# First slab of each normed stage in plain float32 from the residual, and a rebuilt gated recurrence, in a 22-stage network on one core

## The chip, the cores and the metric

The kernel runs on one core of a Trainium2 chip. The metric is the device time of one execution in microseconds. Times are of the whole program, and every time below is from runs of the kernel before the change or from the trace of its profiled execution.

## The reference, cut to what matters

The input is one sequence of 256 tokens of width 1024. It goes through residual blocks: y = x + gate * f(norm(x)). A stage that begins with a norm is called a normed stage here; there are ten. Everything is float32, and the kernel keeps near-float32 accuracy.

```python
def rms_norm(x, g):
    y = x32 * lax.rsqrt(jnp.mean(x32 * x32, axis=-1, keepdims=True) + EPS)
    return y * g
def modulate(x, g, shift, scale):
    return rms_norm_2(x, g) * (1.0 + scale[:, None, :]) + shift[:, None, :]
def rglru_mixer(h, ...):                      # the gated recurrence
    gate, xr = jnp.split(h @ w_in, 2, axis=-1)
    xr = causal_dwconv(xr, conv_w, conv_b)    # 4 taps
    r = sigmoid(xb @ w_a + b_a); i = sigmoid(xb @ w_x + b_x)   # per block of 128
    a = exp(-8 * r * softplus(-lam)); b = sqrt(-expm1(2 log a)) * (i * xr)
    h_t = a_t h_{t-1} + b_t                   # scan over the 256 tokens
    return (gelu(gate) * hs) @ w_out
```

The norm's factor 1/sqrt(mean + eps) is one number for each token, so it may be applied to the matmul's result as well as to its input: (x * g * r) @ W = ((x * g) @ W) * r. With a modulation, shift @ W has to be added after that.

## The kernel before, in words

**Layout.** Activations lie transposed: channels on the 128 partitions, the 256 tokens (T) along the free axis. The residual X is 8 tiles of 128x256 (KD = 8). All weights come from memory as 272 slabs of 128x2048 floats (1 MB), in the order in which the stages use them; slab n goes to raw[n % 4], loaded by SyncE four ahead. N0[stage] is the number of a stage's first slab.

**Three matmuls for one.** TensorE (PE) takes fp32r operands, which hold fewer bits than float32. So every slab is split on chip: ScalarE (ACT) copies it to hi in fp32r (split_hi, L1018, two halves of 128x1024), VectorE (DVE) makes lo = raw - hi (split_lo, L1485, two halves). Activations are split in the same way to XH and XL (after a norm), or HH and HL (hidden values). A product is hi*XH + hi*XL + lo*XH (three, L341 to L343), so a slab of 16 blocks of 128x128 is 48 matmuls of 256 columns. In the stages with a modulation (gated_slab) hi takes XH and XL in one matmul of 512 columns (L410) and lo one of 256 (L412). hi and lo have two buffers (n % 2): slab n+2 can be split once slab n is used.

**A stage boundary.** At the end of a down-projection DVE adds the results to X pair by pair (residual). ACT squares the tiles of X (L1046) into S; DVE folds the first four squares (L1504). norm() on PE then sums squares over channels (12 float32 matmuls of 64 columns, L535, 24 records in the trace, since a float32 matmul is recorded as two), issues 8 matmuls whose result nobody reads (busy, L522), ACT takes the square root (L1051), DVE the reciprocal, and a float32 matmul of 256 columns spreads the factor to all partitions (L543, into bank 4). DVE then makes S = X * gain * factor (L1569), ACT XH (L1057, or L1059 with the shift), DVE XL (L1560, L1562), tile by tile. The stage's first slab (first_up_slab L394 and L402, or gated_stage L439 and L446) follows these tiles as they come. Its hi and lo were made during the residual.

**The recurrence.** Stage rg_in has 10 slabs. Each holds 128 columns of gate and the same 128 of xr side by side. For each slab ACT takes gelu of the gate half (L1240) and starts the convolution of the other (L1244), DVE adds three taps (L1830), PE multiplies by the two block matrices (gates, L685 and L687, float32), ACT takes two tanh (L1230, L1232). After the last slab ACT runs tanh and exp for all ten tiles (L1253, L1256), then all square roots (L1261); DVE then runs product, scan, product, cast and subtraction (L1847 to L1851) tile by tile, and only after the tenth splits the slabs of rg_out. rg_out waits for the values so made (h_ready).

The engines run their own instructions in program order and wait on semaphores. What an engine waits for holds back all that stands behind it.

## Time and profile before

| what | value |
|---|---|
| runs | 1857.72, 1857.73, 1859.61 us, median 1857.73 |
| profiled execution | 1854.29 us, of which the span is 1852.5 us |
| mean granted TensorE clock | 0.982 |
| PE / weight loads / DVE / ACT busy | 96% / 89% / 75% / 53% |
| largest single wait of PE | 20.2 us, before rg_out |

The span is cut in the profile into matmuls (PE), weight loads (PEld) and the other engines. Matmuls overlap their successors in the trace, so a distance from start to start is the cost of one, not its own duration. The granted clock is 1.0 at 2.4 GHz and 0.5 at 1.2 GHz.

### The profile page before, as it was taken

The numbers are of one execution on the slowest core, as the hardware profiler recorded it, in microseconds if no ns is written. First come the engines' busy times: TensorE is split into PE (matmuls) and PEld (weight loads), VectorE is DVE, ScalarE is ACT, GpSimd is POOL, SyncE is SP. The second block draws the span as 40 slices with busy tenths as digits, with TensorE's granted clock in tenths as the row PEclk, the third lists the DMA queues.
The fourth block names the chain that finished last, engine by engine and source line by source line (L and its number), as shares of the span: only waits on it lengthen the run. The fifth ranks groups of instructions, "written<-read, shape, count | busy, mean of one in ns | idle before, by whom it ended". The sixth has DMA issues, their size and how long they took to land.

```text
span 1852.5 us, 31866 instructions
## 1 busy us (share of the span) xinstructions
PE 1770.9 (96%) x12854; PEld 1646.0 (89%) x12854; DVE 1384.8 (75%) x2169; ACT 974.4 (53%) x1495; POOL 16.5 (1%) x22
## 2 busy tenths in 40 slices
PE   7899999948999999999998999999999999899999
PEld 7699999948999988899997698889988999588899
DVE  4668887767888788888975867888788865856663
ACT  5455544562555365536565835553555445655542
POOL 0200000000000000000000000000000000000000
PEclk9999999978999999999999999999999999999999
DMA  8235468422445957795553035779577834035552
GB/s 346 92 109 188 181 228 307 162 99 91 162 181 185 367 201 290 272 350 196 183 182 124 14 128 195 281 282 344 215 282 281 320 141 179 2 113 187 199 182 91
DMA packets 62154, 367.16 MB, mean 198 GB/s; under 512 B 6912, under 2 KB 7040, under 8 KB 27360
## 3 DMA queue, kind: packets, MB, share of 16 engines
q1 hardware_dynamic: 61488, 362.69, 53.0%
q0 software_dynamic: 560, 3.01, 0.4%
q8 instruction: 72, 1.18, 0.3%
q14 instruction: 34, 0.28, 0.0%
HBM read 364.63 MB, written 1.05 MB: 197 GB/s over the span
## 4 chain that ended last, share of the span: by engine, by line
PE 85%; DVE 9%; ACT 4%; issue 1%; DMA 1%; SPq 0%; DVEq 0%; ACTq 0%
PE psum L410 17%; PE psum L341 17%; PE psum L343 16%; PE psum L342 16%; PE psum L412 8%; DVE lo L1485 2%; DVE S L1569 1%; PE psum L394 1%; ACT hi L1018 1%; PE psum L535 1%; DVE XHL L1562 1%; PE psum L733 1%; PE psum L805 1%; DVE tiny L1701 1%; PE psum L402 1%
## 5 line engine op out<-in xcount | busy, mean ns | idle before, releaser
L1485 DVE TENSOR_TENSOR lo<-raw,hi 128x1024 fp32r<-128x1024 f32 x542 | 641.3, 1224 | 247.0 <-ACT hi L1018 246.4
L1018 ACT ACTIVATE hi<-raw 128x1024 fp32r<-128x1024 f32 x542 | 543.3, 1051 | 456.4 <-PE psum L343 431.3
L410 PE MATMUL psum<-XHL,hi 128*128 128x512 f32 x1344 | 471.0, 397 | 1.7 <-DVE lo L1485 1.7
L341 PE MATMUL psum<-XHL,hi 128*128 128x256 f32 x1400 | 399.5, 285 | 2.2 <-DVE lo L1485 2.0
L342 PE MATMUL psum<-XHL,hi 128*128 128x256 f32 x1400 | 396.6, 283 | 0.0
L343 PE MATMUL psum<-XHL,lo 128*128 128x256 f32 x1400 | 396.6, 283 | 0.0
L341 PE MATMUL psum<-HH,hi 128*128 (+1 forms) x1328 | 382.4, 288 | 6.5 <-DVE lo L1485 6.5
L342 PE MATMUL psum<-HL,hi 128*128 (+1 forms) x1328 | 380.2, 286 | 0.0
L343 PE MATMUL psum<-HH,lo 128*128 (+1 forms) x1328 | 380.0, 286 | 0.0
L412 PE MATMUL psum<-XHL,lo 128*128 128x256 f32 x1344 | 375.2, 279 | 0.0
L410 PEld LDWEIGHTS psum<-XHL,hi 128*128 128x128 f32 x1344 | 252.4, 188 | 63.3 <-DVE lo L1485 2.5
L341 PEld LDWEIGHTS psum<-XHL,hi 128*128 128x128 f32 x1400 | 268.9, 192 | 5.4 <-issue 3.0
L342 PEld LDWEIGHTS psum<-XHL,hi 128*128 128x128 f32 x1400 | 268.9, 192 | 0.2
L343 PEld LDWEIGHTS psum<-XHL,lo 128*128 128x128 f32 x1400 | 268.9, 192 | 0.0
L341 PEld LDWEIGHTS psum<-HH,hi 128*128 128x128 f32 x1328 | 259.3, 195 | 7.4 <-issue 6.8
L342 PEld LDWEIGHTS psum<-HL,hi 128*128 128x128 f32 x1328 | 259.3, 195 | 0.1
L343 PEld LDWEIGHTS psum<-HH,lo 128*128 128x128 f32 x1328 | 259.2, 195 | 0.0
L412 PEld LDWEIGHTS psum<-XHL,lo 128*128 128x128 f32 x1344 | 253.5, 189 | 0.0
L1586 DVE CUSTOM_DVE_ANT_0 modw<-modw,cond 128x1024 f32<-128x1024 f32 x144 | 173.9, 1220 | 11.6 <-DMA modw<-wmod_dram 11.6
L1113 ACT ACTIVATE S<-psum 128x512 f32<-128x512 f32 x88 | 52.6, 598 | 220.2 <-PE psum L412 220.2
L1657 DVE TENSOR_TENSOR S<-psum,S 128x512 f32<-128x512 f32 x88 | 60.9, 692 | 72.5 <-ACT S L1113 72.4
L1626 DVE SCALAR_TENSOR_TENSOR S<-psum,PAR,S 128x254 f32<-128x254 f32 (+1 forms) x176 | 72.5, 475 | 0.0
(294 smaller groups left out, 1661.1 us busy)
## 6 DMA issues: line engine op xcount, KB each, us to landing
raw<-slabs_dram SPq DMA_DIRECT2D x270, 1024.0 KB, 4.8
modw<-wmod_dram SPq DMA_DIRECT2D x144, 512.0 KB, 5.7
A<-small_dram POOLq DMA_DIRECT2D x1, 1536.0 KB, 13.2
X<-x_dram SPq DMA_DIRECT2D x4, 256.0 KB, 3.8
raw<-slabs_dram SPq DMA_DIRECT2D x2, 512.0 KB, 6.3
out_dram<-X SPq DMA_DIRECT2D x4, 256.0 KB, 2.4
cond<-cvec_dram POOLq DMA_DIRECT2D x1, 512.0 KB, 7.2
A<-tab_dram POOLq DMA_DIRECT2D x1, 512.0 KB, 15.3
```

The source lines that it names most:

```text
L341: mm(dst, wh, xh, start=start, stop=False, skip_group_check=True)
L342: mm(dst, wh, xl, start=False, stop=False, skip_group_check=True)
L343: return mm(dst, wl, xh, start=False, stop=False, skip_group_check=True)
L394: mm(b[:, m * T:(m + 1) * T], w[:, k, at], XH[:, kt, :], start=(m == 0 and i == 0 and w is hi), stop=False, skip_group_check=True)
L410: mm(dst, hi[:, k, j * P:(j + 1) * P], XHL[:, kt, :, :].rearrange("p a t -> p (a t)"), start=start, stop=False, skip_group_check=True)
L412: return mm(dst[:, T:2 * T], lo[:, k, j * P:(j + 1) * P], XHL[:, kt, 0, :], start=False, stop=False, skip_group_check=True)
L1018: f(hi[:, n % SPLIT, at], raw[:, n % RAW, at], ACT.Copy).then_inc(q["hi_ready"], 1)
L1113: f(S[:, 1024 + s % 2 * 512:1536 + s % 2 * 512].rearrange("p (a t) -> p a t", a=2), psum[:, b:b + 2, T:2 * T], ACT.Copy).then_inc(q["half_ ...
L1485: v.tensor_tensor(lo[:, n % SPLIT, at], raw[:, n % RAW, at], hi[:, n % SPLIT, at].bitcast(F32), ALU.subtract).then_inc(q["lo_ready"], 1)
L1586: v.tensor_tensor_reduce(out=w, in0=w, in1=cond[:, :], scale=1.0, scalar=0.0, op0=ALU.mult, op1=ALU.add, accum_out=MOD[:, n:n + 1]).then_i ...
L1626: last = stt(out=z, in0=bank[n % 4][:, m * T:(m + 1) * T - tap], scalar=col(f"fconv{layer}", (2 - tap) * 44 + k, i, 4), in1=z, op0=ALU.mul ...
L1657: v.tensor_tensor(two(dst), psum[:, b:b + 2, 0:T], two(S[:, 1024 + s % 2 * 512:1536 + s % 2 * 512]), ALU.add).then_inc(evacuated[s % 2], 1)
```

## The change

Slabs in FIRST, the first of each of the ten normed stages, are no longer split. PE multiplies the raw slab, as float32, by XG = X * gain (or by XGS, which also has two columns with the shift, 258 columns in all), 16 matmuls (raw_slab). The sum of squares and the spread stand between them; DVE folds all squares, so the sum takes 4 matmuls instead of 12; the busy matmuls are gone. ACT writes XG between the squares. The spread factor is kept in SBUF (row_kept), and DVE multiplies the first slab's result by it (unscaled); with a shift, ACT then adds it as a bias. The stage's second slab takes the place that the first had: it follows XH and XL tile by tile (paced_slab). hi and lo alternate over split slabs only (SPLITS). The load of slab n+4 behind a slab in FIRST waits for that slab's use instead of its split. pa_in loads 8 columns of parameters ahead of slab 0.

In the recurrence the slabs hold first xr (5 slabs of two tiles) and then the gate (5 slabs). The convolution and the gate matmuls run in the first half; tanh, exp and the arguments of the roots run beside the slabs of the second half; then come five roots, five gelus, scans, products, HH by ACT instead of DVE, and HL, in pairs of tiles, with the splits of rg_out between them.

```diff
+FIRST = [N0[_name] for _name in ("pa_in", "f0_up", "rg_in", "f1_up", "g00_up", "ssd_in", "g01_up", "g10_up",
+                                 "mla_in", "g11_up")]
+SPLITS, HALVED = [], []
+for _n in range(NSLABS):
+    SPLITS.append(len(HALVED))
+    if _n not in FIRST:
+        HALVED.append(_n)
...
+                if n - RAW in FIRST:
+                    sp.wait_ge(q["slab_used"], n - RAW + 1)
+                else:
+                    sp.wait_ge(q["lo_ready"], 2 * (SPLITS[n - RAW] + 1))
+                sp.dma_start(raw[:, k, :], slabs[n]).then_inc(raw_loaded[k], 16)
...
+            def raw_slab(stage, dst, wide=T, bank_of_sums=3):
+
+                n, k = N0[stage], norms[0]
+                norms[0] += 1
+                source = XG if wide == T else XGS
+                sums = bank[bank_of_sums]
+
+                def part(kt, ms=(0, 1)):
+                    pe.wait_ge(q["xg_ready"], KD * k + kt + 1)
+                    for m in ms:
+                        at = slice((m * KD + kt) * P, (m * KD + kt + 1) * P)
+                        last = mm(dst(m), raw[:, n % RAW, at], source[:, kt, 0:wide],
+                                  start=(kt == 0 and (m == 0 or wide > T)), stop=False, skip_group_check=True)
+                    return last
+
+                def column_sums():
+                    pe.wait_ge(q["squares_folded"], k + 1)
+                    for m in range(2):
+                        for j in range(2):
+                            last = mm(sums[:, j * WIDE:(j + 1) * WIDE], S[:, m * T + j * P:m * T + (j + 1) * P],
+                                      ones[:, 0:WIDE], start=(m == 0 and j == 0), stop=False, skip_group_check=True)
+                    last.then_inc(q["sum_ready"], 1)
+
+                def spread():
+                    pe.wait_ge(q["diag_ready"], k + 1)
+                    mm(bank[4][:, 0:T], ones, R[:, 0:T], start=True, stop=True).then_inc(q["spread_ready"], 1)
+
+                if n == 0:
+                    column_sums()
+                    pe.wait_ge(q["slab_begun"], 16)
+                    for kt in range(KD):
+                        part(kt, (0,))
+                    spread()
+                    pe.wait_ge(raw_loaded[0], 16)
+                    for kt in range(KD):
+                        last = part(kt, (1,))
                 else:
-                    pe.wait_ge(q["xh_ready"], KD * (norms[0] - 1) + kt + 1)
...
+                    pe.wait_ge(raw_loaded[n % RAW], 16 * (n // RAW + 1))
                     for kt in range(KD):
...
+                        last = part(kt)
+                        if kt == 2:
+                            column_sums()
+                        if kt == 4:
+                            spread()
...
+                raw_slab(stage, lambda m: psum[:, m, 0:T + 2], T + 2, bank_of_sums)
+                paced_slab(N0[stage] + 1, preps,
+                           lambda m, half, w, x_, first: mm(psum[:, 2 + m, half:half + T], w, x_,
+                                                            start=(first and half == 0), stop=False,
+                                                            skip_group_check=True),
+                           lambda m, w, x_: mm(psum[:, 2 + m, T:2 * T], w, x_, start=False, stop=False,
+                                               skip_group_check=True))
+                pe.wait_ge(q["row_kept"], norms[0])
...
+            def gates(u):
+
+                pe.wait_ge(*up_count("rg_in", u))
+                for t in (2 * u, 2 * u + 1):
+                    if t >= 4:
+                        pe.wait_ge(q["it_ready"], t - 3)
+                    at = t * T
+                    mm(bank[4 + t % 4][:, 0:T], SW[:, 4 + t, :], S[:, at:at + T], start=True, stop=False,
+                       skip_group_check=True)
+                    mm(bank[4 + t % 4][:, T:2 * T], SW[:, 14 + t, :], S[:, at:at + T], start=False,
+                       stop=True, skip_group_check=True).then_inc(q["ri_ready"], 1)
...
+            def split_hi(n, i=None, ahead=False):
+
+                if n in FIRST:
+                    n += 1
+                if n >= NSLABS or n - 2 in FIRST and not ahead:
...
+                if shift is not None:
+
+                    if k:
+                        act.wait_ge(q["resid_ready"], 8 * (k - 1) + 2)
+                    f(XGS[:, :, T:T + 2], MOD[:, at:at + 8].rearrange("p (a t) -> p a t", t=1).to_broadcast([P, KD, 2]),
+                      ACT.Copy)
+
+                def scaled(kt):
+                    if shift is None:
+                        f(XG[:, kt, :], X[:, kt, :], ACT.Copy, scale=col(gain, kt)).then_inc(q["xg_ready"], 1)
+                    else:
+                        f(XGS[:, kt, 0:T], X[:, kt, :], ACT.Copy,
+                          scale=MG[:, at // 3 + kt:at // 3 + kt + 1]).then_inc(q["xg_ready"], 1)
+
                 for m, w in ((0, 2), (2, 2), (4, 2), (6, 1), (7, 1)):
...
+                    if k and m < 6:
+                        scaled(m)
+                        scaled(m + 1)
                 if k == 0:
-                    split_hi(0)
+                    act.wait_ge(q["gain_loaded"], 16)
+                for kt in range(6 if k else 0, KD):
+                    scaled(kt)
                 act.wait_ge(q["sum_ready"], k + 1)
                 f(tiny[:, 52:54], bank[bank_of_sums][:, 0:2 * WIDE:WIDE], ACT.Sqrt, scale=1.0 / D,
                   bias=tiny[:, 59:60]).then_inc(q["norm_ready"], 1)
-                split_hi(N0[stage] + 1)
+                if k == 0:
+                    split_hi(1)
+                else:
+                    split_hi(n + 2, ahead=True)
...
+            def decays(u):
+
+                for t in (2 * u, 2 * u + 1):
+                    f(TH[:, t, :], A1[:, t, :], ACT.Tanh, scale=c4[:, t:t + 1],
+                      bias=c4[:, t:t + 1]).then_inc(q["act_steps"], 1)
+                for t in (2 * u, 2 * u + 1):
+                    act.wait_ge(q["act_steps"], 1 + t + 1)
+                    f(A1[:, t, :], A1[:, t, :], ACT.Exp, scale=c4[:, RNN + t:RNN + t + 1],
+                      bias=c4[:, RNN + t:RNN + t + 1]).then_inc(q["rg_exp"], 1)
...
+                if 1 <= s <= 5:
+                    gate_tanhs(2 * s - 2)
+                    gate_tanhs(2 * s - 1)
+                if s >= 5:
+                    if s == 5:
+                        act.wait_ge(q["it_ready"], RNN)
+                    decays(s - 5)
+            act.wait_ge(q["rg_evacuated"], 5)
+            for u in range(5):
+                act.wait_ge(q["rg_arg"], u + 1)
+                f(TH[:, 2 * u:2 * u + 2, :], TH[:, 2 * u:2 * u + 2, :], ACT.Sqrt).then_inc(q["rg_root"], 1)
+            for u in range(5):
+                f(GG[:, 2 * u:2 * u + 2, :], GG[:, 2 * u:2 * u + 2, :],
+                  ACT.Gelu_apprx_tanh).then_inc(q["rg_gate"], 1)
+            for u in range(5):
+                act.wait_ge(q["rg_state"], u + 1)
+                f(HH[:, 2 * u:2 * u + 2, :], GG[:, 2 * u:2 * u + 2, :], ACT.Copy).then_inc(q["rg_high"], 1)
+                if u >= 2:
+                    split_hi(N0["rg_out"] + u)
+            split_hi(N0["rg_out"] + 5)
+
...
+            def unscaled(z, banks):
+
+                dve.wait_ge(q["row_kept"], norms[0])
+                row = R[:, T:2 * T].rearrange("p (a t) -> p a t", a=1).to_broadcast([P, 2, T])
+                return v.tensor_tensor(two(z), banks, row, ALU.mult)
...
+                for m in tiles:
+                    dve.wait_ge(q["squares_ready"], 8 * k + m + 2)
+                    last = v.tensor_tensor(S[:, 0:2 * T], S[:, 0:2 * T], S[:, m * T:(m + 2) * T], ALU.add)
+                    if m == 6:
+                        last.then_inc(q["squares_folded"], 1)
+                    else:
+                        step.link(last)
...
+                split_lo(N0[stage] + (2 if k else 1), halves=(0,), ahead=True)
...
+            def scans(u):
+                dve.wait_ge(q["rg_root"], u + 1)
+                step.link(v.tensor_tensor(tiles(TH, u), tiles(TH, u), tiles(IX, u), ALU.mult))
+                for t in (2 * u, 2 * u + 1):
+                    last = v.tensor_tensor_scan(IX[:, t, :], A1[:, t, :], TH[:, t, :], 0.0, ALU.mult, ALU.add)
+                step.put(last)
+
+            def product(u):
+                dve.wait_ge(q["rg_gate"], u + 1)
+                step.wait(step.n)
+                v.tensor_tensor(tiles(GG, u), tiles(GG, u), tiles(IX, u), ALU.mult).then_inc(q["rg_state"], 1)
+
+            def rest(u):
+                dve.wait_ge(q["rg_high"], u + 1)
+                v.tensor_tensor(tiles(HL, u), tiles(GG, u), tiles(HH, u).bitcast(F32),
+                                ALU.subtract).then_inc(q["h_ready"], 1)
+
+            scans(0)
+            scans(1)
+            product(0)
+            product(1)
+            for u in range(5):
+                rest(u)
+                if u >= 2:
+                    split_lo(N0["rg_out"] + u)
+                if u + 2 < 5:
+                    scans(u + 2)
+                    product(u + 2)
```

First place: PE at the boundary from f1_down to g00_up, the fifth norm. `CN,S` is the sum of squares, `R,CN` the spread. Before:

```order
L343 MATMUL psum<-HH,lo 128x256
L535 MATMUL psum<-CN,S 128x64 [waits squares_folded]
L535 MATMUL psum<-CN,S 128x64 x3
...
L522 MATMUL psum<-maskr,identr 128x256 x8
L543 MATMUL psum<-R,CN 128x256 [waits diag_ready]
L522 MATMUL psum<-maskr,identr 128x256 x4
L439 MATMUL psum<-XHL,hi 128x256 [waits xh_ready,lo_ready]
```

Now, at the same place:

```order
L362 MATMUL psum<-HH,lo 128x256
L411 MATMUL psum<-XGS,raw 128x258 [waits xg_ready,raw_loaded1]
...
L419 MATMUL psum<-CN,S 128x64 [waits squares_folded]
L419 MATMUL psum<-CN,S 128x64 x3
L411 MATMUL psum<-XGS,raw 128x258 [waits xg_ready]
...
L425 MATMUL psum<-R,CN 128x256 [waits diag_ready]
L411 MATMUL psum<-XGS,raw 128x258 [waits xg_ready]
...
L504 MATMUL psum<-XHL,hi 128x256 [waits xh_ready,lo_ready]
```

Six of the sixteen float32 matmuls stand ahead of the sum, four between sum and spread, six behind the spread; what waited for XH there is now the second slab.

Second place: DVE at the same boundary, from the reciprocal on. Before:

```order
L1552 TENSOR_SCALAR R<-CN,tiny 128x128
L1569 SCALAR_TENSOR_TENSOR S<-X,MG,psum 128x256 [waits spread_ready]
...
L1562 SCALAR_TENSOR_TENSOR XHL<-S,MOD,XHL 128x256 [waits xh_ready] x3
L1485 TENSOR_TENSOR lo<-raw,hi 128x1024 [waits hi_ready] x2
L1657 TENSOR_TENSOR S<-psum,S 128x512 [waits half_kept]
```

Now:

```order
L1726 TENSOR_SCALAR R<-CN,tiny 128x128
L1647 TENSOR_TENSOR lo<-raw,hi 128x1024 [waits hi_ready]
L1744 SCALAR_TENSOR_TENSOR S<-X,MG,psum 128x256 [waits spread_ready]
...
L1737 SCALAR_TENSOR_TENSOR XHL<-S,MOD,XHL 128x256 [waits xh_ready] x3
L1647 TENSOR_TENSOR lo<-raw,hi 128x1024 [waits hi_ready]
L1654 TENSOR_TENSOR S<-psum,R 128x512 [waits row_kept,half_kept]
```

One half of a slab's split went ahead of the wait for the spread, the other stayed behind the tiles, and it is now the stage's third slab that it belongs to.

Third place: ACT from the last gate slab of the recurrence to the first values for rg_out. Before, the tail of it:

```order
L1256 ACTIVATE A<-A,c 128x256 [waits act_steps]
L1261 ACT_TABLE_LOAD
L1261 ACTIVATE S<-S 128x256 [waits rg_arg] x10
L1018 ACTIVATE hi<-raw 128x1024 [waits slab_used,raw_loaded1]
```

Now:

```order
L1079 ACTIVATE hi<-raw 128x1024
L1391 ACTIVATE GG<-psum 128x512 [waits slab_used]
L1367 ACTIVATE TH<-A,c 128x256 x2
L1371 ACTIVATE A<-A,c 128x256 [waits act_steps] x2
L1403 ACT_TABLE_LOAD [waits rg_arg]
L1403 ACTIVATE TH<-TH 128x512 [waits rg_evacuated]
L1403 ACTIVATE TH<-TH 128x512 [waits rg_arg] x4
L1405 ACT_TABLE_LOAD
L1405 ACTIVATE GG<-GG 128x512 x5
L1409 ACTIVATE HH<-GG 128x512 [waits rg_state] x3
L1079 ACTIVATE hi<-raw 128x1024 [waits slab_used,raw_loaded1]
```

Eight of the ten tanh and exp pairs went ahead beside the slabs; the gelus and the copies to HH joined the tail.

## Rows read from the trace of the kernel before

**Rows 1.** Page, the chain that ended last: shares of the span by engine.
```profile
PE 85%; DVE 9%; ACT 4%; issue 1%; DMA 1%; SPq 0%; DVEq 0%; ACTq 0%
```

**Rows 2.** Windows from a stage's last matmul to its successor's third slab; after the colon: length, busy time by engine.
```profile
318.91:337.63 18.72, 17.80 (x141) 16.95 (x140) 14.86 (x30) 11.31 (x21) 0.00 (x0) 1.00 0.37 143
456.77:474.56 17.79, 17.04 (x137) 16.37 (x136) 14.90 (x31) 11.09 (x20) 0.00 (x0) 1.00 0.36 126
653.36:671.69 18.33, 16.94 (x121) 15.46 (x120) 15.64 (x30) 11.68 (x20) 0.00 (x0) 1.00 0.36 121
846.22:864.99 18.77, 17.12 (x137) 16.35 (x136) 16.75 (x35) 11.64 (x20) 0.00 (x0) 1.00 0.34 129
...
sum 165.35, PE 153.74 PEld 144.19 DVE 138.06 ACT 101.40 POOL 0.00; mean PE 17.08 PEld 16.02 DVE 15.34 ACT 11.27 POOL 0.00
```

**Rows 3.** Timeline of PE at g00_up: start us, us, what, idle before.
```profile
654.65 2.00 PE L535 MATMUL psum<-CN,S 128*128 128x64 f32 x16 [0.17 <-ACT S L1046]
...
657.72 0.70 PE L543 MATMUL psum<-R,CN 128*128 128x256 f32 x2
```

**Rows 4.** Timeline of ACT at the same boundary.
```profile
650.01 1.28 ACT L1039 ACT_TABLE_LOAD   x1
...
651.41 1.14 ACT L1046 ACTIVATE S<-X 128x512 f32<-128x512 f32 x2
...
658.98 1.31 ACT L1059 ACTIVATE XHL<-S,MOD 128x256 fp32r<-128x256 f32 x3
```

**Rows 5.** Timeline of DVE at the same boundary.
```profile
652.58 0.69 DVE L1504 TENSOR_TENSOR S<-S 128x512 f32<-128x512 f32 x1 [1.02 <-ACT S L1046]
...
658.46 1.26 DVE L1569 SCALAR_TENSOR_TENSOR S<-X,MG,psum 128x256 f32<-128x256 f32 x3 [0.79 <-PE psum L543]
...
663.58 1.27 DVE L1562 SCALAR_TENSOR_TENSOR XHL<-S,MOD,XHL 128x256 fp32r<-128x256 f32 x3
664.77 2.35 DVE L1485 TENSOR_TENSOR lo<-raw,hi 128x1024 fp32r<-128x1024 f32 x2
```

**Rows 6.** Timeline of PE: float32 matmuls of 256 columns, then fp32r ones.
```profile
389.93 0.60 PE L685 MATMUL psum<-S,A 128*128 128x256 f32 x2
390.36 0.59 PE L687 MATMUL psum<-S,A 128*128 128x256 f32 x2
...
430.99 0.28 PE L342 MATMUL psum<-HL,hi 128*128 128x256 f32 x1
431.11 0.28 PE L343 MATMUL psum<-HH,lo 128*128 128x256 f32 x1
```

**Rows 7.** Waits of PE from 390 to 440 us: us in total, times, longest.
```profile
PE psum L495 <- DVE HL L1851: 20.2, 1, 20.2
PE psum L341 <- DVE lo L1485: 5.6, 1, 5.6
PE psum L685 <- DVE S L1830: 4.2, 1, 4.2
```

**Rows 8.** Timeline of ACT in the recurrence's tail.
```profile
410.15 0.60 ACT L1256 ACTIVATE A<-A,c 128x256 f32<-128x256 f32 x1
410.76 1.28 ACT L1261 ACT_TABLE_LOAD   x1
412.06 3.17 ACT L1261 ACTIVATE S<-S 128x256 f32<-128x256 f32 x10
```

**Rows 9.** Timeline of DVE in the recurrence: three taps.
```profile
393.55 1.51 DVE L1830 SCALAR_TENSOR_TENSOR S<-psum,PAR,S 128x255 f32<-128x255 f32 x3
```

**Rows 10.** Windows in rg_out; the number behind the five engines is the granted clock.
```profile
418.00:422.00 4.00, 4.00 (x21) 4.00 (x21) 3.76 (x10) 0.00 (x0) 0.00 (x0) 0.50 0.00 0
436.00:444.00 8.00, 6.97 (x37) 7.00 (x38) 4.29 (x4) 0.00 (x0) 0.00 (x0) 0.58 0.58 230
```

**Rows 11.** Timeline of ACT and PE at the program's start: split of slab 1, use of slab 1.
```profile
13.96 2.00 ACT L1018 ACTIVATE hi<-raw 128x1024 fp32r<-128x1024 f32 x2 [0.81 <-DMA raw<-slabs_dram]
...
23.61 0.28 PE L341 MATMUL psum<-XHL,hi 128*128 128x256 f32 x1
```

More of the change, by code:

```diff
@@ L991, in _ @@
                       next_spread, key_ready)
-            up_stage("mla_out", 12)
-            norm(6)
-            gated_stage("g11_up", 13)
+            paced_up(N0["mla_out"], 12, shift=MLA_SHIFT)
+            for s in range(1, 4):
+                up_slab("mla_out", s)
+            pe.wait_ge(q["resid_ready"], RESID["mla_out"] + 4)
+            gated_stage("g11_up", 13, 6)
             down_stage("g11_down")
@@ L1279, in _ @@
             act.wait_ge(q["mod_ready"], 2)
-            norm("ssd_in", 0, 24, then=ACT.Silu)
+            norm("ssd_in", None, 0, 24, then=ACT.Silu)
             def ssd_silu(c):
@@ L1462, in _ @@
             act.wait_ge(q["mod_ready"], 6)
-            norm("g11_up", 1, 48, 6, ACT.Silu)
+            norm("g11_up", None, 1, 48, 6, ACT.Silu)
             gated_ffn("g11_up")
```

494 lines of the change are left out of this document (270 added, 224 removed).

## The prediction

> **What bounds the kernel now.** I read the chain that ended last first. It is PE for 85% of the span, DVE for 9% and ACT for 4% [rows 1], so time is won where PE waits or works for nobody. The windows show where, at the stage boundaries. From the last matmul of a stage to the first of the next stage's third slab pass 18.33 us at g00_up and 18.77 us at ssd_in, and 165.35 us in all nine boundaries after the first norm [rows 2]. Two slabs take 48 matmuls each, and fp32r matmuls of 256 columns start 0.12 us apart [rows 6]: 11.5 us. The other 6 to 7 us are norm sums, filler matmuls and waits.
>
> The timeline of PE at g00_up shows one such wait: the sums end at 656.65, and the spread starts only at 657.72 [rows 3]. The list of waits adds the recurrence: 20.2 us ahead of rg_out, 5.6 us inside it for a split that DVE has behind its scans, 4.2 us for the last taps [rows 7].
>
> **A boundary with the change.** I set zero at the start of the last matmul, 653.36 for g00_up [rows 2].
>
> The price of the float32 slab comes first. Two float32 matmuls of 256 columns start at 389.93 and 390.36, 0.43 us apart [rows 6]. Sixteen are 6.9 us, against 5.8 us for the 48 fp32r ones. So the slab costs 1.1 us more of PE and saves only by being early. The trace has no 258-column form; it is taken at the same price, the 2 columns in 256 are 0.05 us a slab.
> The page "FP8 and Floating Point Precision" of the Trainium skill (TensorE Precision Notes) counts four passes for true float32. At the 0.12 us of an fp32r pass that would be an estimate of 7.7 us a slab, 7 us more over ten slabs than by the rows; the trace has the duration, and it is used.
>
> Is XG there in time? ACT starts its table load at 650.01, that is at -3.35, and the squares follow 1.4 us later [rows 4]. The shift columns (128x16) are not in the trace; between nothing and the 0.4 us of a 128x256 form I take 0.1, since they are nearer to nothing. A square of 128x512 takes 0.51 us start to start, a 128x256 activation with an operand 0.40 (two in the first 0.80 us of the 1.31 that three take) [rows 4]. Three rounds of one square and two XG are 3.9 us, two single squares 0.6 us: the last square ends near 2.7. XG 0 to 2 are ready by 0.6, so PE starts at 0.1 and has done six matmuls at 2.7. Then it meets a wait: the sum needs the fold of the last squares, 0.69 us on DVE [rows 5] and a handshake, so 3.6. Cost 0.9 us of PE.
> Sums: 8 records at 0.12 us [rows 3], to 4.5. Four float32 matmuls, to 6.2. The spread waits for root, reciprocal and diagonal, 1.07 us behind the sums (656.65 to 657.72) [rows 3], so it is ready; 0.4 us, to 6.6. Six more, to 9.2. Second slab 5.8, to 15.0.
> Is the second slab fed? DVE's first scaled tile followed the spread by 0.74 us and the last XL ended 6.4 us later [rows 3, 5]. Now that is 6.95 and 13.35. The last three matmuls of the second slab would want it at 14.5. Fed. The third slab needs both halves of its split, and the second half stands behind the tiles: 1.15 us [rows 5], 14.5 against 15.0. That is the thinnest cover: 0.5 us. One microsecond lost in the DVE chain costs about half a microsecond per boundary, two cost 1.5. The first half of the split, 1.15 us, hides in the wait for the spread. unscaled (0.7 us, like the 128x512 fold) and ACT's row copy come behind the tiles, and who waits for them is the convolution or gate of the first slab. Its buffers are wanted by PE only four slabs on.
>
> So a boundary with a modulation takes 15.0 us instead of 18.33 to 18.77; without one (no shift, cheaper copies) 14.7 instead of about 17.7. In ssd_in DVE goes from the tiles to eight taps of the first slab before it splits slab 3, which I place 0.7 us late. mla_in loses 0.4 us, since the result of its first slab passes DVE and ACT once more. Eight boundaries without the recurrence were 165.35 - 18.72 = 146.6 us [rows 2]. Now 14.7 twice, 14.9 at g11_up (residual early), 15.0 at three, 15.7 and 15.4: 120.4. **Gain 26.2 us.** The held load of slab n+4 is issued at 9.2 and not wanted before the second of the later slabs is used, near 20: hidden.
>
> **The recurrence.** Before, from the last matmul ahead of it at 318.91 to the last of rg_out at 456.77 pass 137.9 us [rows 2]. Now, from zero: raw slab to 8.9, second slab to 14.7. gates(0) needs the taps of the first slab, which DVE can begin only behind tiles, split and unscaled, at 14.5, and behind two linear copies of ACT, at 15.5. Six taps at 0.42 (0.50 with the links between them [rows 9]): 18.0. **A new wait of 3.3 us.** Then five gates at 4 x 0.43 = 1.7 us and eight slabs at 5.76: PE ends rg_in at 72.8.
> Behind the last slab ACT splits one slab (2.0 us), copies (0.5), runs two tanh and two exp (2.2), loads a table (1.28) [rows 4, 8, 11], takes five roots of 128x512 (0.53 each, as the squares), loads again (1.28), runs five gelus (2.7) and the first HH (0.6): 13.2. DVE subtracts: first value at 14.0, PE resumes near 14.2, instead of 20.2. The next pairs come every 2.7 us (product, two scans, product, subtraction, at 0.65 an operation of 512 columns or a scan), faster than PE's 5.8 a slab, and the splits stand between them, so the wait of 5.6 is gone.
> The clock: behind the wait of 20.2 the granted clock was 0.50, the lower of its two levels (1.2 GHz), and 21 matmuls stand in 4 us instead of 33. Behind the wait of 5.6 it was 0.58 over 8 us, where 37 stand in 7 busy us instead of 58: 2.5 us lost [rows 10]. The first loss comes again, the second doesn't. rg_out is 28.8 us for five slabs and 2.3 of clock. Sum 72.8 + 14.2 + 31.1 = 118.1. **Gain 19.8 us**, its boundary included.
> The page "ScalarE: Activation LUTs" (What ACT_TABLE_LOAD costs) adds a drain of 1.38 us to each load. In the trace the root follows the load's end within 0.02 us (412.06 after 412.04) [rows 8]. By the page the two loads in the tail would cost 2.8 us more.
>
> **The start.** Slab 0 as float32 runs while the clock is low, but PE isn't the limit. Slab 1 is split after it lands (13.96) [rows 11], later by the issue of one more DMA (0.45 us). DVE now does half of its split ahead of the tiles, eight tiles at 0.72, the other half behind: both halves at 23.8 to 24.0, when slab 1 began at 23.61 before [rows 11]. PE meanwhile is idle for 4 to 5 us, about as long as the 5.6 of [rows 7] that was followed by the low clock. The loss lies between 0.3 (no drop) and 2.8 us (the 2.5 above on top). I take **1.5**.
>
> **Sum.** 26.2 + 19.8 - 1.5 = 44.5 us. The profiled execution was 1854.3, so its like becomes 1809.8. The median of the runs is 3.4 us above it: **1813**. A difference under 0.2% (3.7 us) can't be told from none.
>
> **Bounds.** XG tile: 0.36 to 0.51 us, over eight tiles +-1 us in the last square, so +-0.8 a boundary, 7 in all. The new waits in the recurrence: 0 to 6 us, and its tail +-2. The start 0.3 to 2.8.
>
> **Rivals.**
> *DVE takes PE's place.* The tiles end later than 13.35, the third slab waits for its lo, and 1 to 2 us of each boundary's gain are lost. For it: the cover of 0.5 us, and DVE is busy 16.75 of 18.77 us at ssd_in [rows 2]. Against: nothing was added ahead of the tiles that isn't in a wait. 9 x 1.3 = 12 us less: 1825. Chance 0.2.
> *The recurrence keeps its idle time.* ACT slips in the second half (its 4.8 us of 5.76 a slab are near full), or the tail's roots and gelus come later: 8 to 10 us less, 1822. Chance 0.08.
> *More is won.* The sum doesn't wait, the clock stays up at start and in rg_out: 4 + 1 + 3 us, 1805. Chance 0.1.
> *Float32 matmuls don't overlap with fresh weights.* One record lasts 0.38 us by itself; rows 6 show pairs of 0.60 us from first start to last end, so they overlap there, but with weights that stood in SBUF long before. At 2 x 0.38 a slab would take 12.1 us: ten times 5.2 more, 1865, slower. It decides from 11.4 us a slab. Chance 0.02.
> *No change,* because two of these come together at the boundaries: 0.01.
> Forecast 0.59. The range reaches from the case of more gain to the first rival: 1802 to 1829. Faster 0.96, same 0.01, slower 0.03.
>
> **What would show it.** The sixteen raw matmuls in 6.9 us plus one gap near 0.9 ahead of the sum; the third slab at 15.0; a gap of 3 us ahead of the first gates and one of 14 ahead of rg_out; slab 1 near 24. The forecast is wrong if a raw matmul costs over 0.5, or if PE waits for lo ahead of the third slab, or for the taps more than once in the recurrence.

## The result, and the profile after

| | before | after |
|---|---|---|
| runs | 1857.72 to 1859.97 us (4), median 1858.67 | 1817.08 to 1817.83 us (4), median 1817.65 |
| profiled execution, its span | 1854.29 us, 1852.5 us | 1817.08 us, 1815.3 us |
| mean granted clock | 0.982 | 0.987 |
| PE / weight loads / DVE / ACT busy | 96% / 89% / 75% / 53% | 96% / 89% / 75% / 55% |

The ratio is 0.9778, with a 95% interval of 0.9761 to 0.9795: 41 us faster. The forecast of 1813 lies 4.7 us below, the range of 1802 to 1829 holds the result.

The chain that ended last is still PE's. The part that fell most is DVE's, from the 9% of [rows 1]; ACT's rose from 4% to 6%:

```profile
PE 84%; DVE 7%; ACT 6%; issue 1%; DMA 0%; SPq 0%; DVEq 0%; ACTq 0%
```

The windows of [rows 2], cut at the same places (a stage's last matmul, the start of its successor's third slab; after the colon the length, then busy time by engine, the granted clock, DMA share and GB/s):

```profile
317.74:339.48 21.74, 17.75 (x101) 15.69 (x100) 19.03 (x39) 15.45 (x31) 0.00 (x0) 0.90 0.39 148
439.27:454.33 15.06, 14.37 (x94) 13.14 (x92) 13.30 (x28) 10.93 (x24) 0.00 (x0) 1.00 0.29 111
633.13:648.33 15.20, 14.43 (x94) 13.14 (x92) 13.57 (x28) 11.44 (x25) 0.00 (x0) 1.00 0.29 112
825.40:840.20 14.80, 14.43 (x93) 13.13 (x92) 13.41 (x28) 11.05 (x24) 0.00 (x0) 1.00 0.31 116
...
sum 142.37, PE 133.05 PEld 120.77 DVE 127.29 ACT 103.91 POOL 0.00; mean PE 14.78 PEld 13.42 DVE 14.14 ACT 11.55 POOL 0.00
```

The sum holds nine boundaries, as in [rows 2]. Without the recurrence's 21.74 it is 120.6 us, where the forecast had 120.4. PE at g00_up shows how such a boundary runs now, and answers to [rows 3]:

```profile
633.13 0.28 PE L362 MATMUL psum<-HH,lo 128*128 128x256 f32 x1
633.25 2.78 PE L411 MATMUL psum<-XGS,raw 128*128 128x258 f32 x12
636.80 1.10 PE L419 MATMUL psum<-CN,S 128*128 128x64 f32 x8 [0.77 <-DVE S L1673]
637.74 1.96 PE L411 MATMUL psum<-XGS,raw 128*128 128x258 f32 x8
639.53 0.59 PE L425 MATMUL psum<-R,CN 128*128 128x256 f32 x2
639.97 2.77 PE L411 MATMUL psum<-XGS,raw 128*128 128x258 f32 x12
642.39 0.47 PE L504 MATMUL psum<-XHL,hi 128*128 128x256 f32 x1
```

A float32 matmul has two records, so six matmuls, the column sums, four, the spread, six. The waits of PE in the recurrence's stage, beside [rows 7] (us in total, times, longest):

```profile
PE psum L556 <- DVE HL L2057: 13.9, 1, 13.9
PE psum L726 <- DVE S L2027: 3.3, 1, 3.3
PE psum L419 <- DVE S L1673: 0.7, 1, 0.7
```

The waits of 5.6 and 4.2 us are gone, that of 20.2 is 13.9, and 3.3 us are new. Where the time went by stage follows from four profiles: lengths from the start of one stage's last matmul to that of the next one's, in us (the last stage to the end of the span).

| stage | before | before again (e7) | after | after again (e1) | gain forecast |
|---|---|---|---|---|---|
| start | 122.45 | 123.03 | 123.88 | 124.76 | -1.5 |
| f0 | 196.47 | 196.46 | 193.86 | 193.86 | 3.0 |
| recurrence | 137.86 | 137.84 | 121.53 | 121.58 | 19.8 |
| f1 | 196.59 | 196.58 | 193.86 | 193.86 | 3.1 |
| g00 | 192.87 | 195.87 | 192.27 | 191.87 | 3.3 |
| ssd | 275.53 | 275.63 | 271.27 | 271.67 | 3.1 |
| g01 | 195.35 | 195.33 | 191.61 | 191.61 | 3.7 |
| g10 | 195.34 | 195.34 | 191.87 | 191.87 | 3.7 |
| mla | 143.47 | 140.71 | 139.29 | 139.30 | 3.4 |
| g11 | 196.54 | 198.77 | 195.85 | 195.84 | 3.1 |

The two profiles of before differ, by 2 to 3 us in g00, mla and g11, though the program is the same. That is taken up with e7. By e7 against e1 the recurrence gave 16.3 us, the eight stages behind the other boundaries 24.8, the start took 1.7: 39.3 us, against 44.5 forecast.

### The profile page after: what moved, and what is told of

It reads as the page before. It is cut to its first block, busy times and chain, and to the rows that moved or that the text cites. A ratio compares the mean times of both kernels' runs of the same rounds, so it can differ in the third digit from the quotient of the medians.

```text
span 1815.3 us, 31256 instructions
## 1 busy us (share of the span) xinstructions
PE 1748.4 (96%) x12490; PEld 1619.3 (89%) x12490; DVE 1368.6 (75%) x2130; ACT 996.7 (55%) x1583; POOL 16.6 (1%) x22
## 4 chain that ended last, share of the span: by engine, by line
PE 84%; DVE 7%; ACT 6%; issue 1%; DMA 0%; SPq 0%; DVEq 0%; ACTq 0%
PE psum L482 17%; PE psum L360 16%; PE psum L362 16%; PE psum L361 16%; PE psum L484 8%; ACT hi L1079 2%; DVE lo L1647 2%; PE psum L411 1%; PE psum L472 1%; ACT S L1122 1%; PE psum L504 1%; PE psum L789 1%; ACT XGS L1113 1%; PE psum L866 1%; DVE S L1744 1%
## 5 line engine op out<-in xcount | busy, mean ns | idle before, releaser
L1647 DVE TENSOR_TENSOR lo<-raw,hi 128x1024 fp32r<-128x1024 f32 x522 | 618.5, 1224 | 226.3 <-ACT hi L1079 226.1
L1079 ACT ACTIVATE hi<-raw 128x1024 fp32r<-128x1024 f32 x522 | 522.9, 1051 | 408.2 <-PE psum L362 385.5
L482 PE MATMUL psum<-XHL,hi 128*128 128x512 f32 x1280 | 452.5, 399 | 0.0
L360 PE MATMUL psum<-XHL,hi 128*128 128x256 f32 x1304 | 371.6, 285 | 2.2 <-DVE lo L1647 2.2
L361 PE MATMUL psum<-XHL,hi 128*128 128x256 f32 x1304 | 369.4, 283 | 0.0
L362 PE MATMUL psum<-XHL,lo 128*128 128x256 f32 x1304 | 369.3, 283 | 0.0
L484 PE MATMUL psum<-XHL,lo 128*128 128x256 f32 x1280 | 359.5, 281 | 0.0
L482 PEld LDWEIGHTS psum<-XHL,hi 128*128 128x128 f32 x1280 | 240.5, 188 | 59.8
L360 PEld LDWEIGHTS psum<-XHL,hi 128*128 128x128 f32 x1304 | 250.7, 192 | 4.5 <-issue 4.2
L361 PEld LDWEIGHTS psum<-XHL,hi 128*128 128x128 f32 x1304 | 250.8, 192 | 0.2
L362 PEld LDWEIGHTS psum<-XHL,lo 128*128 128x128 f32 x1304 | 250.6, 192 | 0.0
L484 PEld LDWEIGHTS psum<-XHL,lo 128*128 128x128 f32 x1280 | 241.8, 189 | 0.0
L1809 DVE SCALAR_TENSOR_TENSOR S<-psum,PAR,S 128x255 f32<-128x255 f32 (+1 forms) x168 | 69.1, 474 | 0.0
```

Source lines behind the costliest of these rows:

```text
L360: mm(dst, wh, xh, start=start, stop=False, skip_group_check=True)
L361: mm(dst, wh, xl, start=False, stop=False, skip_group_check=True)
L362: return mm(dst, wl, xh, start=False, stop=False, skip_group_check=True)
L482: mm(dst, hi[:, k, j * P:(j + 1) * P], XHL[:, kt, :, :].rearrange("p a t -> p (a t)"), start=start, stop=False, skip_group_check=True)
L484: return mm(dst[:, T:2 * T], lo[:, k, j * P:(j + 1) * P], XHL[:, kt, 0, :], start=False, stop=False, skip_group_check=True)
L1079: f(hi[:, k % SPLIT, at], raw[:, n % RAW, at], ACT.Copy).then_inc(q["hi_ready"], 1)
```

## The experiments

They were run in three groups. In these the runs of before had medians of 1857.37, 1856.97 and 1856.95 us. All edits start from the changed kernel, and "the stage" is the recurrence's, 121.55 us there.

**e1, the changed kernel again.**

> The changed kernel itself, timed on the chip of the runs beside it: 1817 to 1818 us. In its trace the modulated slabs (one matmul of 512 columns and one of 256 per block) again take 5.65 us each in all four stages, if their rhythm is a property of the kernel; if it is chance, one of the stages takes 5.55.

1817.38 us (1816.00 to 1820.16), ratio 0.978 (0.9761 to 0.98). The modulated slabs take 5.65 us each in all four stages again. The stages repeat within 0.1 us, but for the start (0.9 us longer) and g00 and ssd, which differ by 0.4.

**e2, the old recurrence under raw first slabs.** The slabs of the recurrence again hold both halves of a tile, with gates, scans and products as before; its first slab stays raw.

```diff
             raw_slab("rg_in", lambda m: bank[N0["rg_in"] % 4][:, m * T:(m + 1) * T])
-            for s in range(1, RNN):
...
-                if s <= 5:
-                    gates(s - 1)
+            paced_up(N0["rg_in"] + 1, 4)
+            gates(0)
+            for s in range(2, RNN):
+                up_slab("rg_in", s)
+                gates(s - 1)
+            gates(RNN - 1)
```

> The change without the rebuilt recurrence: slabs with gate and xr side by side again, first one in float32. Theory: the two parts add up. The profiles give 16.3 us for rg_in and rg_out together, of which the float32 slab alone is 3, so this kernel is 12 to 14 us slower than the changed one, 1830 to 1832 us. Rival: the rebuild only moves the wait (3.3 us ahead of the first gates, 14 ahead of rg_out), then under 5 us slower, below 1823. With 20 us of wait ahead of rg_out and 5.6 in it, as before.

1835.39 us (1834.18 to 1836.04), ratio 0.9876 (0.9858 to 0.9893), so 18.0 us above e1 and 3 to 5 above what was expected. The stage takes 138.05 us, no less than before: here the raw slab is worth nothing. The waits of PE in it say why:

```profile
PE psum L556 <- DVE HL L2017: 20.2, 1, 20.2
PE psum L360 <- DVE lo L1618: 6.4, 1, 6.4
PE psum L726 <- DVE S L1996: 6.4, 2, 4.2
```

Against [rows 7] the wait for lo grew by 0.8 us and the gates have a second wait of 2.2 us, since DVE comes to the taps of the first slab only behind tiles, split and unscaled. Behind that wait the granted clock is low for 3.4 us as well. The third slab starts 18.91 us behind zero, against the 18.72 of [rows 2]. So without the rebuild the raw slab gains nothing in this stage. The run splits the whole gain: 22.0 us of it (from 1857.37 to 1835.39) are there with the raw slabs alone, 18.0 come with the rebuild on top. The rebuild with a split first slab was not run, so what it would give by itself is not shown.

**e3, the first gates one slab later.**

```diff
-                if s <= 5:
+                if s == 2:
+                    gates(0)
+                if 2 <= s <= 5:
                     gates(s - 1)
```

> The first gates of the recurrence go behind the third slab, ahead of the second gates; nothing else changes. Theory: the wait of 3.3 us for the taps and the low clock that follows it (335.2 to 342.0 us) both cost, 3 us each, and the taps are ready by the end of the third slab: 5 to 6 us faster than the changed kernel, 1812. Rival: the wait moves to the second gates or to the splits behind the later tanh on ScalarE: 0 to 2 us, 1816 to 1818.

1813.07 us (1812.86 to 1815.60), ratio 0.976 (0.9742 to 0.9778). The stage takes 115.63 us, 6.0 less than in e1, and 0.4 us are left of the new wait:

```profile
PE psum L556 <- DVE HL L2059: 13.9, 1, 13.9
...
PE psum L726 <- DVE S L2029: 0.4, 1, 0.4
```

That is more than the wait of 3.3 us. In the changed kernel the row behind it shows the rest: the first gates' matmuls, and the start of the third slab.

```profile
336.26 1.22 PE L726 MATMUL psum<-S,A 128*128 128x256 f32 x2 [3.30 <-DVE S L2027]
337.28 1.06 PE L728 MATMUL psum<-S,A 128*128 128x256 f32 x2
...
339.49 0.78 PE L360 MATMUL psum<-XHL,hi 128*128 128x256 f32 x1
```

They take 3.2 us where four float32 matmuls at the 0.43 us of [rows 6] would take 1.7. The windows of 336 to 340 and 340 to 344 us have granted clocks of 0.50 (the lower of the two levels, 1.2 GHz) and 0.75.

**e4, the wait filled.** The wait stays, but 26 matmuls that nobody reads stand in it.

```diff
+                if s == 1:
+                    busy(26, 0)
                 if s <= 5:
                     gates(s - 1)
```

> 26 matmuls of 256 columns whose result nobody reads fill the wait ahead of the first gates (3.1 of its 3.3 us). Theory: the clock does not fall there, so the gates take 1.7 instead of 3.2 us and the slab behind them 5.8 instead of 7: 2.5 to 3 us faster, 1815. Rival: the low clock costs nothing because VectorE or ScalarE set the pace of those slabs: no change, 1817.5.

1815.60 us (1815.07 to 1816.32), ratio 0.977 (0.9753 to 0.9786). The stage takes 118.52 us, 3.0 less than in e1, and the clock stays up (length, busy time by engine, granted clock):

```profile
332.00:344.00 12.00, 11.80 (x92) 11.39 (x91) 8.77 (x16) 6.76 (x12) 0.00 (x0) 1.00 0.71 285
```

By this split the wait itself costs 2.9 us (118.52 to e3's 115.63), and the low clock behind it 3.0. One caution came with e11 below, which has the same wait, nothing in it, and the clock up:

```profile
335.80 0.70 PE L727 MATMUL psum<-S,A 128*128 128x256 f32 x2 [3.30 <-DVE S L2028]
336.34 0.59 PE L729 MATMUL psum<-S,A 128*128 128x256 f32 x2
```

Seven profiles have this wait, of 3.3 or (e5, e6) 4.2 to 4.3 us. The clock is low behind it for 6.8 us in five of them (after, e1, e6, e8, e9), for 3.4 in e5, and not at all in e11. e2 has a shorter one there, of 2.2 us, with 3.4 us of low clock behind it. So the size of the clock's share is shown: e4 and e11, with the clock up, start the third slab 20.17 and 20.16 us behind zero, the other six of the seven at 21.3 to 22.7. That the filler kept it up in e4 is likely but, after e11, not shown.

**e5, column sums and spread one round later.**

```diff
-                        if kt == 2:
+                        if kt == 3:
                             column_sums()
-                        if kt == 4:
+                        if kt == 5:
                             spread()
```

> The column sums of a raw slab come behind its fourth round (eight matmuls) instead of its third (six), and the spread behind its sixth instead of its fifth. The changed kernel's PE waits 0.7 us ahead of the sums in each of nine boundaries, for the fold of the squares. Theory: with two raw matmuls (0.86 us) put into that wait it is gone, and the third slab starts 0.7 us earlier: 9 x 0.7 = 6.3 us, near 1811. Rival: the third slab's start hangs on DVE, whose tiles start with the spread: the spread then comes no earlier (6.4 us behind zero), the tiles end at the same time, and if PE already runs into their end, the 0.7 us come back as a wait for lo ahead of the third slab: about 1817.

1812.85 us (1811.78 to 1815.12), ratio 0.9762 (0.9745 to 0.9778), 4.5 us below e1 of the 6.3 expected. Each of the eight boundaries outside the recurrence gains 0.8 to 0.9 us (third slab at 14.20 instead of 15.06, 14.33 instead of 15.20), and so the theory holds for the boundaries. ssd takes 275.05 us, 3.4 more. One wait of PE grew in it, that of the fourth slab, 1.0 us in e1:

```profile
PE psum L360 <- DVE lo L1647: 1.9, 1, 1.9
```

There the rival holds: DVE has eight taps ahead of that split, and the 0.9 us that PE wins ahead of it comes back as a wait, so that the fourth slab starts 22.14 us behind zero in both runs. The 3.4 us by which the stage is longer go with the clock, low for 17.1 us of it in three pieces, against 6.8 in two in e1. The recurrence gains no boundary either: its wait ahead of the gates is 4.2 us instead of 3.3, and the 1.9 us by which it is shorter go with less low clock (17.1 us of it instead of 23.9).

**e6, the whole split behind the tiles.**

```diff
-                split_lo(N0[stage] + (2 if k else 1), halves=(0,), ahead=True)
+                if k == 0:
+                    split_lo(1, halves=(0,), ahead=True)
...
-                split_lo(N0[stage] + (2 if k else 1), halves=(1,), ahead=True)
+                split_lo(N0[stage] + (2 if k else 1), halves=(0, 1) if k else (1,), ahead=True)
```

> The first half of the third slab's split, which DVE does in the wait for the spread, goes behind the tiles, as the second half does (the first boundary of the program is left as it is). This adds 1.15 us to DVE between the tiles' end (near 13.35 us behind zero) and the second half. By my prediction's claim that the third slab needs both halves (second half then at 15.65, wanted at 14.95 to 15.2), PE waits 0.5 to 0.7 us in each of seven to eight boundaries: 4 to 5 us slower, near 1822. Rival: the third slab's first eight rounds need the first half alone (14.5, still ahead of 14.95), the second only 2.8 us later: no wait, 1817 to 1818, and the cover was thicker than I gave.

1821.20 us (1820.31 to 1822.12), ratio 0.9808 (0.9792 to 0.9824). The time is that of the first theory, and the mechanism is not. Outside the recurrence the third slabs start at 14.93 to 15.21 us, as in e1: no wait there. (In the recurrence the wait for the first gates grew, from 3.3 to 4.3 us, but the stage is only 0.1 us longer.) What grew is the wait for the fourth slab in ssd, here, and below it e1's row:

```profile
PE psum L360 <- DVE lo L1647: 1.8, 1, 1.8
```

```profile
PE psum L360 <- DVE lo L1647: 1.0, 1, 1.0
```

ssd takes 2.4 us more than in e1 and mla 1.0. In mla a wait of PE 22 us behind zero (for DVE's HL) goes from 0.4 to 1.4 us. The rest of ssd's is the low clock again (13.6 us of it instead of 6.8).

**e7, the kernel before again.** No edit.

> The kernel before, profiled once more. In its first profile the modulated slabs of two stages (g00_up, g11_up) took 5.55 us each and those of two others 5.65 us, at the same granted clock; twenty slabs a stage, so 2.1 us a stage. In all profiles of changed kernels all four stages take 5.65. The first profile's execution was 4.4 us below the median of the last runs of before. Theory: the pace is drawn anew at each stage of each execution, behind the wait of 0.4 us that stands ahead of it; this profile shows another mixture, and its time less the median goes with it (2.1 us a stage at 5.55). Rival: the pace belongs to the program; then g00_up and g11_up have 5.55 again.

1857.37 us, span 1855.6. The modulated slabs alternate matmuls of 512 and of 256 columns. In the first profile of before, 672 such matmuls (21 slabs) stand in these windows of g00_up and of g01_up:

```profile
666.05:782.50 116.45, 116.45 (x671) 101.75 (x672) 101.02 (x128) 62.86 (x84) 0.00 (x0) 1.00 0.75 280
1134.67:1253.40 118.73, 118.73 (x672) 103.00 (x672) 100.73 (x125) 62.84 (x84) 0.00 (x0) 1.00 0.74 275
```

and in the second one in this window of g00_up:

```profile
666.60:785.30 118.70, 118.70 (x672) 102.95 (x672) 101.10 (x128) 62.83 (x84) 0.00 (x0) 1.00 0.74 275
```

The clock is 1.00 in all. One program, one stage, 116.45 us in one execution and 118.70 in the next: the pace doesn't belong to the program, and the rival falls. That it is drawn stage by stage fits; that the wait of 0.4 us ahead of the stage has a part in it is not shown, and e11 tests it. g11_up went from 5.55 to 5.65 us a slab as well; mla's 143.47 us became 140.71, with the clock at 1.00 from 1627.2 to 1634.0 us, where it had been low. So my profile of before was 4.5 us short by two quick stages (118.70 - 116.45, twice) and 2.8 us long by one loss of clock. The other 0.8 us by which g00 differs are not explained here. All the profiles of the changed kernel and its variants have 5.65 in the four stages.

**e8, the start's wait filled.**

```diff
                     for kt in range(KD):
                         last = part(kt, (1,))
+                    for kt in range(8):
+                        last = mm(bank[5][:, 0:T], raw[:, 0, kt * P:(kt + 1) * P], XG[:, kt, :],
+                                  start=True, stop=True)
```

> Eight float32 matmuls that nobody reads stand in the wait of 3.7 us between the raw slab 0 and slab 1 of the first stage. In the changed kernel the granted clock is low from 24.6 to 28.0 us behind that wait. Theory: the wait stays as long, but the clock stays up, and the first stage is 1.4 us shorter: near 1816. Rival: the start is bounded by DVE's tiles and splits and not by PE's clock, since slab 2 wants its split late too: within 0.3 us of the changed kernel.

1818.06 us (1812.72 to 1818.56), ratio 0.978 (0.9763 to 0.9798): no gain. The clock stays up at the start, as meant, but is low for longer later on (here the windows of e8):

```profile
24.00:30.00 6.00, 5.65 (x47) 5.66 (x48) 3.16 (x4) 2.01 (x3) 0.00 (x0) 1.00 1.01 418
80.20:93.90 13.70, 13.70 (x46) 8.36 (x47) 9.29 (x26) 6.72 (x24) 0.00 (x0) 0.50 0.00 0
```

and of e1:

```profile
25.50:28.90 3.40, 3.40 (x19) 3.40 (x18) 1.38 (x2) 1.24 (x2) 0.00 (x0) 0.51 0.99 405
83.60:90.40 6.80, 6.80 (x22) 4.04 (x23) 6.22 (x18) 3.40 (x12) 0.00 (x0) 0.50 0.00 0
```

The theory was right for the place and wrong for the stage, which takes 125.23 us against 124.76. Whether the end of the one low stretch brought the length of the other is open: e10 and e12 have the long one without the short one too, but e3 has both.

**e9, two HH copies behind the third and the fourth gelu.**

```diff
-            for u in range(5):
-                f(GG[:, 2 * u:2 * u + 2, :], GG[:, 2 * u:2 * u + 2, :],
-                  ACT.Gelu_apprx_tanh).then_inc(q["rg_gate"], 1)
+            for u in range(3):
+                gelu_of(u)
             for u in range(5):
                 act.wait_ge(q["rg_state"], u + 1)
                 f(HH[:, 2 * u:2 * u + 2, :], GG[:, 2 * u:2 * u + 2, :], ACT.Copy).then_inc(q["rg_high"], 1)
+                if u < 2:
+                    gelu_of(3 + u)
```

> In ACT's tail of the recurrence the first two HH copies stand behind the third and the fourth gelu instead of behind the fifth. The first product is there at 405.15 (87.4 us behind the stage's zero), so the first HH can end at 406.0 instead of 407.0 and the first HL at 406.7 instead of 407.7. Theory: rg_out starts 1.0 us earlier and the whole stage is 1.0 us shorter: near 1816.4. Rival: rg_out's first slab is paced by its later pairs (DVE's scans and products), which aren't earlier; what is won at the start is lost inside the first slab: no change.

1818.56 us (1815.40 to 1820.04), ratio 0.979 (0.9774 to 0.9806): not to be told from e1. The wait ahead of rg_out is 12.9 us instead of 13.9, as expected, and the stage is 2.2 us shorter (119.38), the second microsecond by 13.7 us of low clock instead of 17.1. The profile gives it back in g00, 1.8 us, where DVE waited for the weights of the modulation:

```profile
DVE modw L1768 <- DMA modw<-wmod_dram: 6.3, 5, 2.7
...
PE psum L360 <- DVE lo L1652: 1.1, 3, 0.5
```

In e1 that wait of DVE is 3.4 us over the same stretch. The tail's edit doesn't touch those transfers, so I take this as spread between executions; one profile can't tell.

**e10, the edits of e3, e5 and e9 together.**

> The gates one slab later, the sums and the spread one round later, and ACT's tail reordered, all three. By the single runs: gates -6.0 us in the recurrence's stage, tail -1.0 to -2.2 there, sums -0.85 in each of the eight boundaries and 1 to 4 us lost again in ssd_in, where DVE has the fourth slab's split behind eight taps. If they add: 1817.4 - 6.0 - 1.5 - 6.8 + 2.5 = 1805.6. If the tail and the gates share one loss of clock, or sums and gates the same wait of DVE: 1808 to 1810.

1811.28 us (1809.51 to 1812.47), ratio 0.9751 (0.9738 to 0.9764). That is above both expected values (1805.6 and 1808 to 1810). The recurrence's stage takes 113.89 us, 7.7 less than in e1, where e3, e5 and e9 gained 6.0, 1.9 and 2.2 alone. Not all of that adds: the sums' 0.9 us goes into the wait that e3 had left (1.3 us instead of 0.4), and the gains by less low clock overlap. The whole is 6.1 us below e1, not 12: ssd is 3.0 us longer (as in e5), mla 2.8.

**e11, a pause of PE ahead of the modulated slabs.**

```diff
                 pe.wait_ge(q["row_kept"], norms[0])
+                pe.wait_ge(q["slab_used"], N0[stage] + 2)
                 for s in range(2, 4):
                     gated_slab(stage, s)
```

> The changed kernel, with PE waiting for the end of its own second slab before it starts the modulated slabs of the four stages. Before, a wait of 0.4 us for lo stood at this place, and two of four stages ran at 5.55 us a slab; in the changed kernel PE comes without a gap and all run at 5.65. Theory: a PE that starts the alternation of 512 and 256 columns from rest can fall into the quick pace; the wait costs 0.4 us a stage, and each stage that falls into it gains 2.1: 1813 to 1815 if two to four do. Rival: the gap ahead has nothing to do with it: 1819.

1817.09 us (1816.28 to 1820.24), ratio 0.9789 (0.9774 to 0.9804). All four stages run at 5.65 us a slab, and each starts its third slab 0.27 us later. The theory has no support here: the pause alone doesn't bring the quick pace. The time lies between the two expected ones. It was seen in two of 56 modulated stages in 14 profiles, both in one execution of before.

**e12, e10 with that pause.**

> All three edits of the run together, and the wait of the run before on top. If the wait brings the quick pace, 3 to 6 us below the run with the three edits alone; if not, 1.6 us above it.

1807.74 us (1804.93 to 1809.04), ratio 0.9735 (0.9722 to 0.9749): the fastest of all, and its runs lie below all of e10's. It is 3.5 us below e10, as expected for the quick pace, but by luck: the pace is 5.65 us again. The pause costs 0.3 us in three of the stages, but ssd is 3.05 us shorter than in e10 and mla 4.3. The clock does it: it is low for 6.8 us of ssd and 3.4 of mla, where e10 has 17.1 and 13.7, and PE falls behind e12 in e10 at those places alone. Windows of e10, at two places where it was low:

```profile
1032.40:1042.60 10.20, 7.81 (x34) 6.92 (x35) 6.06 (x21) 1.89 (x3) 0.00 (x0) 0.50 0.01 2
1585.40:1592.20 6.80, 6.11 (x28) 3.82 (x25) 0.85 (x2) 1.43 (x4) 0.00 (x0) 0.50 0.32 133
```

and of e12 near the first and at the second:

```profile
1029.10:1039.30 10.20, 7.63 (x35) 5.92 (x36) 7.42 (x25) 2.61 (x6) 0.00 (x0) 0.67 0.01 2
1585.40:1592.20 6.80, 6.80 (x59) 6.80 (x59) 0.54 (x2) 1.31 (x2) 0.00 (x0) 1.00 0.01 4
```

Why a shift of a microsecond moves these losses stays open. Small edits ahead of ssd and mla change the time by 2 to 4 us in this way, without having anything to do with those stages.

## Why the prediction was right, and where it was not

**The boundaries: right, the sum by some luck.** At g00_up the sixteen raw matmuls take 0.44 us each, with sums at 3.7 us (forecast 3.6), spread at 6.4 (6.2), the second slab at 9.3 (9.2), the third at 15.20 (15.0). The wait ahead of the sums is 0.77 us where I had 0.9. The terms of the eight boundaries were off by 0.4 us on one side (f0 and f1, late) to 0.9 on the other (ssd_in, early), and their sum by 0.2, since these cancel. The price of a float32 matmul, taken from two rows of another stage, carried over to fresh weights and 258 columns, so the rival at 1865 fell. The Trainium skill's four passes for float32 (page "FP8 and Floating Point Precision", TensorE Precision Notes), at 0.12 us each, would make 0.48 us a matmul; the rows above have 0.44, in two records. (Over ten slabs that estimate is 8 us above the rows' price, not the 7 that I wrote.)

**What the boundaries gave the stages: less than I summed.** 26.0 us at the boundaries became 24.8 in the stages (e7 against e1). The part missing most is in mla, which won 3.6 us at its third slab and kept 1.4: PE has a new wait there, of 0.4 us for DVE's HL, and meets the low clock for 6.8 us (from 1509.4 on in the first profile), where e7 has 3.4 us of it. In ssd the fourth slab waits 1.0 us for its split; I had allowed 0.7 for that.

**The cover of 0.5 us: wrong.** I wrote that the third slab needs both halves of its split. It needs the first, which DVE does ahead of the tiles, and the second only 2.9 us after its start. DVE's rows in g00_up, answering to [rows 5]:

```profile
639.18 1.23 DVE L1647 TENSOR_TENSOR lo<-raw,hi 128x1024 fp32r<-128x1024 f32 x1 [0.26 <-ACT hi L1079]
640.32 1.26 DVE L1744 SCALAR_TENSOR_TENSOR S<-X,MG,psum 128x256 f32<-128x256 f32 x3
...
645.43 1.27 DVE L1737 SCALAR_TENSOR_TENSOR XHL<-S,MOD,XHL 128x256 fp32r<-128x256 f32 x3
646.62 1.22 DVE L1647 TENSOR_TENSOR lo<-raw,hi 128x1024 fp32r<-128x1024 f32 x1
```

The second half ends at 647.84 and is wanted near 651.2: a cover of 3.3 us. e6 moved 1.15 us into it and, outside the recurrence, no third slab waited. So the rival in which DVE takes PE's place had its place wrong. DVE does take it, but at the fourth slab of ssd and in mla, where convolution taps, or work on the stage's first slabs, stand ahead of what PE wants next.

**The recurrence: the mechanism right, 3.4 us too short.** The stage took 121.5 us, not 118.1. The gates came 18.5 us behind zero (18.0), after the wait of 3.3 us that I had forecast. The step that failed is the one behind it, "five gates at 4 x 0.43 = 1.7 us and eight slabs at 5.76". I had priced a loss of clock behind the long wait and for the start, and none behind this one. The first gates took 3.2 us, and the matmuls behind them were slow up to 342 us: 2.8 us of the 3.4. e4 measures the clock's share as 3.0. The tail was right: ACT's rows, answering to [rows 8],

```profile
398.49 1.28 ACT L1403 ACT_TABLE_LOAD   x1
399.78 2.71 ACT L1403 ACTIVATE TH<-TH 128x512 f32<-128x512 f32 x5
402.51 1.28 ACT L1405 ACT_TABLE_LOAD   x1
403.80 2.71 ACT L1405 ACTIVATE GG<-GG 128x512 f32<-128x512 f32 x5
406.42 1.13 ACT L1409 ACTIVATE HH<-GG 128x512 fp32r<-128x512 f32 x2
```

and PE waits 13.9 us (14.2), rg_out takes 31.5 (31.1). The root starts 0.01 us behind the load's end, the gelu too, and each load starts within 0.02 us of the end of what stood ahead of it, so the drain of 1.38 us that the Trainium skill adds to a load (page "ScalarE: Activation LUTs", What ACT_TABLE_LOAD costs) isn't seen here either.

**The start: right, as far as can be told.** 1.4 us by the first profiles, 1.7 by the second, 1.5 forecast. The low clock was there (3.4 us of it), after a wait of 3.7 us. But over the eleven profiles that have the changed start as it is (all but e8) it took 123.4 to 125.2 us, and in the two of before 122.5 and 123.0, so that the agreement to 0.2 us is luck.

**The baseline.** I summed against one profiled execution and added its 3.4 us to the median at the end. That execution was no plain one: 4.5 us short and 2.8 us long for reasons that e7 shows to change between executions. By the medians the change is worth 41 us (40.0 in the group of e1), by the second profiles 39.3 (1857.37 and 1818.06). Against the 44.5 of the forecast these lack 5.2 us: 3.5 in the recurrence, 1.4 in the eight stages, 0.2 in the start. The forecast of the time was low by 4.7, which is within what such draws make of it.

## What to carry to other kernels

A matmul that can start from unnormalised data pays by being early, even at a higher price of its own (6.9 to 7.0 us a slab instead of 5.8 here); e2 shows that it pays nothing where the next engine's first work on its result comes too late, so move that work in the same edit. Price a new wait of PE as the wait plus the loss of clock that may follow it (here 2.9 and 3.0 us), and look first for the place one slab later, which cost nothing (e3). Where an expected gain of under 4 us is missing in the total, compare stage by stage over two profiles before believing either: gains of one stage went here with clock lost in stages far behind (e5, e10).

## What the hardware showed that I had not expected

- Alternating matmuls of 512 and 256 columns run at one of two steady paces, 5.55 or 5.65 us for 32 of them, at a granted clock of 1.00 in both. A stage keeps its pace from its first slab to its last. At 5.55 the starts in g00_up of before are 230 to 234 and 111 to 119 ns apart, at 5.65 (e7) every third pair is longer (241 and 120 ns). What draws it is open; a pause ahead of the stage isn't enough (e11).
- Float32 matmuls of 256 and of 258 columns cost the same within 0.01 us, and start 0.43 and 0.44 us apart with weights that were never used before.
- The clock was low behind a wait of 3.3 us in most executions and not in all, and removing one such loss (e8) or moving a stage by a microsecond (e12) made others come or go.
